# ScalarE and VectorE in the last two chunks of an expert trip: the next trip's weight units one by one

## What is computed

```python
def moe_swiglu(x, g, w_router, w_eg, w_eu, w_ed):
    h = rms_norm(x, g)
    hf = h.reshape(-1, D_MODEL)                     # (288, 1024)
    ...                                             # combine: two of eight experts per token
    for e in range(N_EXPERTS):                      # 8
        he = jax.nn.silu(hf @ w_eg[e]) * (hf @ w_eu[e])     # (., 3584)
        y = y + combine[:, e:e + 1] * (he @ w_ed[e])        # (., 1024)
    return x + y.reshape(x.shape)
```

## Time and profile before

| | |
|---|---|
| profiled execution, own time | 1645.57 us |
| its span | 1643.8 us |
| median of three runs | 1644.33 us |
| TensorE (PE) busy | 1548.1 us, 94% |
| VectorE (DVE) busy | 1243.2 us, 76% |
| ScalarE (ACT) busy | 971.6 us, 59% |
| share of PE in the chain that ended last | 85% |
| mean granted TensorE clock | 0.966 |
| expert loads (`land`, L310) | 336 of 1024 KB, median 6.0 us from issue to landing |

### The profile page before, as it was taken

The page is one execution under the profiler, slowest core; times in us unless marked ns, Lnnn a source line. Parts: engine busy times, 40 slices in busy tenths (PEclk is TensorE's granted clock), DMA queues, the critical chain, the costliest instruction groups (busy, mean ns, idle before and its releaser), DMA issues.

```text
span 1643.8 us, 22314 instructions
## 1 busy us (share of the span) xinstructions
PE 1548.1 (94%) x7942; PEld 1299.9 (79%) x7942; DVE 1243.2 (76%) x1293; ACT 971.6 (59%) x1086; POOL 87.8 (5%) x85
## 2 busy tenths in 40 slices
PE   6997999999978899989989999999998998998997
PEld 5986999999846778868868877877886887886886
DVE  6995545456774368878888878878887888887885
ACT  6554443345453446766667666667676676666674
POOL 1001110012210100000000000000000000000000
PEclk8999999999977889999999999999999999999999
DMA  8930345445340279969979969987997997997992
GB/s 330 191 96 29 128 165 180 154 167 185 114 175 1 80 274 355 360 273 377 358 276 391 356 253 393 347 340 307 339 363 291 362 363 286 370 361 262 382 357 106
DMA packets 64324, 431.40 MB, mean 262 GB/s; under 512 B 7862, under 2 KB 10166, under 8 KB 13713
## 3 DMA queue, kind: packets, MB, share of 16 engines
q1 hardware_dynamic: 57312, 412.38, 65.6%
q0 software_dynamic: 3616, 12.28, 3.2%
q10 hardware_dynamic: 3344, 6.05, 1.1%
HBM read 422.55 MB, written 9.14 MB: 263 GB/s over the span
## 4 chain that ended last, share of the span: by engine, by line
PE 85%; DVE 5%; issue 5%; ACT 3%; DMA 1%; POOL 1%; DVEq 0%; ACTq 0%; POOLq 0%
PE bank L332 25%; PE bank L334 24%; PE bank L333 24%; PE bank L370 3%; ACT w_hi L1021 2%; PE bank L722 1%; DVE w_lo L1414 1%; PE bank L354 1%; PE bank L588 1%; DVE oe_lo L1563 1%; PE bank L700 1%; PE bank L701 1%; PE bank L668 0%; PE bank L577 0%; PE bank L674 0%
## 5 line engine op out<-in xcount | busy, mean ns | idle before, releaser
L1414 DVE TENSOR_TENSOR w_lo<-land,w_hi 128x2048 fp32r<-128x2048 f32 x224 | 504.1, 2288 | 108.1 <-ACT w_hi L1021 106.5
L1021 ACT CAST w_hi<-land 128x2048 fp32r<-128x2048 f32 x224 | 417.6, 1913 | 3.5 <-issue 3.5
L332 PE MATMUL bank<-w_hi,xe_hi 128*128 128x512 f32 x896 | 370.7, 414 | 16.0 <-DVE xe_lo L1500 16.0
L333 PE MATMUL bank<-w_lo,xe_hi 128*128 128x512 f32 x896 | 358.3, 400 | 0.0
L334 PE MATMUL bank<-w_hi,xe_lo 128*128 128x512 f32 x896 | 357.8, 399 | 0.0
L1024 ACT CAST d_hi<-land 128x2048 fp32r<-128x2048 f32 x112 | 214.1, 1913 | 142.5 <-PE bank L334 142.5
L1511 DVE TENSOR_TENSOR d_lo<-land,d_hi 128x2048 fp32r<-128x2048 f32 x112 | 256.7, 2292 | 28.9 <-ACT d_hi L1024 22.3
L332 PEld LDWEIGHTS bank<-w_hi,xe_hi 128*128 128x128 f32 x896 | 170.3, 190 | 52.6 <-issue 18.5
L334 PEld LDWEIGHTS bank<-w_hi,xe_lo 128*128 128x128 f32 x896 | 170.7, 190 | 41.6
L332 PE MATMUL bank<-d_hi,heT_hi 128*128 128x512 f32 x448 | 179.9, 402 | 18.8 <-DVE heT_lo L1540 18.8
L333 PEld LDWEIGHTS bank<-w_lo,xe_hi 128*128 128x128 f32 x896 | 171.2, 191 | 32.7
(11 more groups left out here) (241 smaller groups left out, 2137.0 us busy)
## 6 DMA issues: line engine op xcount, KB each, us to landing
land<-in_w_expert SPq DMA_DIRECT2D x336, 1024.0 KB, 6.0
land<-in_w_dense SPq DMA_DIRECT2D x54, 1024.0 KB, 4.9
rel_rows<-rb POOLq DMA_DIRECT2D x1, 3072.0 KB, 35.9
bias<-rel_rows ACTq DMA_DIRECT2D x4, 512.0 KB, 4.9
X<-in_x SPq DMA_DIRECT2D x4, 288.0 KB, 5.9
out_y<-X SPq DMA_DIRECT2D x2, 576.0 KB, 4.2
Us<-in_state POOLq DMA_DIRECT2D x1, 1088.0 KB, 9.3
out_conv_s<-Us POOLq DMA_DIRECT2D x1, 1088.0 KB, 8.4
```

What stands on the lines that cost most here:

```text
L332: pe.matmul(out, w[0], x[0], start=start, stop=False)
L333: pe.matmul(out, w[0], x[1], start=False, stop=False)
L1021: act.copy(w_hi[n % RING][:], land[(DENSE + u) % LAND][:]).then_inc(hi_done, 1)
L1414: dve.tensor_tensor(w_lo[n % RING][:], land[slot][:], w_hi[n % RING][:].bitcast(F32), ALU.subtract).then_inc(split, 1)
```

## The change

In chunks 12 and 13 of a trip ScalarE and VectorE do the same operations in another order. Nothing is added or taken away.

- Unit (14,0): ScalarE makes its `hi` before `heT_hi(12)` instead of after it. On VectorE its `lo` stays behind `heT_lo(12)`.
- Unit (14,1): moved out of chunk 12 into chunk 13, behind `xe_split` and `xe_rest`.
- Unit (15,0): from behind `heT_hi(13)` and `heT_lo(13)` to ahead of them, right after (14,1).
- Unit (15,1): on ScalarE from behind `silu(14)`, the next trip's first gate, to ahead of it; on VectorE from behind `gated(14)` to ahead of it.

```diff
@@ ScalarE @@
                         with act.If(trip < n_trips - 1):
                             xe_split((trip + 1) * 2, 0)
                             xe_split((trip + 1) * 2, 1)
+                            expert_hi(trip, NCH, 1)
+                            expert_hi(trip, NCH + 1, 0)
+                    if ch + 2 == NCH:
+                        with act.If(trip < n_trips - 1):
+                            expert_hi(trip, NCH, 0)
                     act.wait_ge(heT_done, trip * NCH + ch + 1)
                     act.wait_ge(d_used, trip * NCH + ch + 2)
                     act.copy(heT_hi[:], bank[6][:, 0:CH]).then_inc(heT_hi_ready, 1)
                     if ch + 2 < NCH:
                         expert_hi(trip, ch + 2, 0)
                         expert_hi(trip, ch + 2, 1)
-                    elif ch + 2 == NCH:
+                    elif ch + 1 == NCH:
                         with act.If(trip < n_trips - 1):
-                            expert_hi(trip, ch + 2, 0)
-                            expert_hi(trip, ch + 2, 1)
-                    else:
-                        with act.If(trip < n_trips - 1):
-                            expert_hi(trip, ch + 2, 0)
+                            expert_hi(trip, NCH + 1, 1)
                             silu(trip, NCH)
-                            expert_hi(trip, ch + 2, 1)
                             expert_hi(trip, NCH, 2)
@@ VectorE @@
                             xe_rest((trip + 1) * 2, 0)
                             xe_rest((trip + 1) * 2, 1)
+                            expert_lo(trip, NCH, 1)
+                            expert_lo(trip, NCH + 1, 0)
                     dve.wait_ge(heT_hi_ready, trip * NCH + ch + 1)
                     dve.tensor_tensor(heT_lo[:], bank[6][:, 0:CH], heT_hi[:].bitcast(F32),
                                       ALU.subtract).then_inc(heT_ready, 1)
@@
                     elif ch + 2 == NCH:
                         with dve.If(trip < n_trips - 1):
-                            expert_lo(trip, ch + 2, 0)
-                            expert_lo(trip, ch + 2, 1)
+                            expert_lo(trip, NCH, 0)
                     else:
                         with dve.If(trip < n_trips - 1):
-                            expert_lo(trip, ch + 2, 0)
+                            expert_lo(trip, NCH + 1, 1)
                             gated(trip, NCH)
-                            expert_lo(trip, ch + 2, 1)
                             expert_down_lo(trip, NCH)
```

## The result

The changed kernel takes 1599.71 us as median of four runs (1598.93 to 1600.99); the kernel before, 1644.96 in runs beside it. The ratio is 0.9726, with a 95% interval of 0.9709 to 0.9743: 45 us, or 2.7%, faster.

What follows compares the result with a forecast made beforehand. TensorE's two waits per boundary, and the clock drops on them, bound the kernel. From 1645.6, seven boundaries save 31.3 us and eight drops 11.9: 1602.4, about 1601 from the median, stated as 1602; range 1597 to 1617.

Steps and rivals of the forecast that it cites:

- First wait gone: Ahead of `gate_up(14,0)`: both `xe_lo` halves ready before TensorE is free at 705.54, so its wait for the tokens disappears.
- (14,1) is late next, 0.2 us: VectorE's rest of (14,1) ends at 708.5; TensorE can go at 708.7, wants to at 708.48: 0.2 us new wait.
- (15,0) and (15,1) at no cost: Ahead of heT(13) and the gate: (15,0) costs nothing, with 0.26 us to spare before `down(13)`, the thinnest cover.
- Second wait 0.5 us: Ahead of `down(14)`: it starts at 720.69 against 720.0 without any wait; remaining waits are 0.2 and 0.5 us.
- Eight drops gone, 11.9 us: At TensorE's waits in the trips: all eight falls of the clock to 0.50 vanish, 8 x 1.49 = 11.9 us.
- Loads: Load queue: (2,2) goes out 6.1 us earlier; the queue's rest falls from 9.5 us a trip to some 2.
- that the drops stay: Rival on TensorE's clock: something besides the wait decides the drops, so they remain; 1614 us, chance 0.13.
- that the second wait stays: Rival at `down(14)`: the hand-over chain on VectorE loses 2 us, only the first wait goes; 1621 us, chance 0.08.
- that the loads bind: Rival on the load queue: a slow load comes 1.4 us late, 1612 us; at 358 GB/s 1615; chance 0.07.
- that `heT_lo(13)` comes late: Rival at `down(13)`: (15,0) not landed in time holds `heT_lo(13)`, making the kernel slower; 1649 us, chance 0.05.

## Why the prediction was right

It said 1602 us, 1597 to 1617; 1599.7 was measured. Point by point:

- *First wait gone.* So it is. The forecast had both halves of `xe_lo` 0.3 us and more ahead of TensorE; the second ends at 703.90, 0.41 ahead of the matmul at 704.31.
- *(14,1) is late next, 0.2 us.* It isn't: TensorE goes on at 707.25, right behind the turn. Its rest, of 2.29 us from 704.89, ends at 707.18, and the matmul starts 0.07 later. I had put 0.23 for this hand-over, read off a matmul that had been waiting, and so made a wait out of nothing; also the rest began 0.07 us before my time for it, shifted by the 1.23.
- *(15,0) and (15,1) at no cost.* Right, and thin as said: `heT_lo(13)` ends at 709.72 and `down(13)` starts without a wait at 710.14. The run with three units shows the price when the cover is gone.
- *Second wait 0.5 us.* 0.50. In sum 0.5 us remain a boundary instead of 0.7, a period is 4.66 us shorter than the undropped one before instead of 4.47.
- *Eight drops gone, 11.9 us.* Right, and shown to follow from the waits by filling them.
- *Loads.* The forecast gave them a rest of 2 us; it is 2.5. No wait of ScalarE for a landing shows. The rate over the periods is 351 to 358 GB/s, with 426 in the catching up. The Trainium skill (HBM Reference, Specifications (TRN2)) gives 358 GB/s for a core when both cores of a domain stream, by which I had worked out 1615. It did not bind this core, as 426 shows; no run here has both cores of a domain at work.

The sum by the trace: 7 x 4.66 = 32.6 and 11.9 for the drops, 44.5 of the 45.7 us between the two profiled executions. The other 1.2 us lie ahead of the first boundary, where `down(12)` ends 1.23 us earlier, though no instruction that TensorE waits for has moved there. They are luck and not the change. The first trip starts while the clock is still at 0.50; the windows from its first matmul to the clock's return, before and after, are:

```profile
581.09:585.99 4.90, 4.90 (x12) 3.88 (x13) 2.89 (x2) 1.35 (x2) 0.00 (x0) 0.50 0.94 366
580.67:583.75 3.08, 3.08 (x7) 2.48 (x8) 2.89 (x2) 1.36 (x2) 0.00 (x0) 0.50 0.86 330
```

The trip starts 0.42 us earlier, and the clock comes back 3.08 us into it instead of 4.90, which makes the stretch up to `down(12)`'s last matmul 123.41 us instead of 124.22. Run again, the changed kernel has 4.09 and 123.83 us. Over all twelve profiles the return lies 2.94 to 5.36 us into the trip, and this stretch grows with it from 123.33 to 124.42 us, whatever the kernel. In the first run with (15,2) moved the return came at 5.36, which makes 1.0 us more than in the changed kernel's profile and fits its gain of less than 2.5 us.

The rivals: that the drops stay, that the second wait stays, that the loads bind, and that `heT_lo(13)` comes late each had their row in the profile, and none shows it. Two of these waits were made to happen by an edit: the second one with (15,1) behind the gate, 24.6 us over the changed kernel where 1626 was expected and 1624.3 came, and a late `heT_lo(13)` with three units ahead, 15 us, near the lower end of the 1613 to 1624 expected.

## What to carry to other kernels

Where one engine waits at two places of a boundary and its helpers idle between them, look for work of the next stage that fits the idle stretch, and place it in whole pieces by the time at which each piece is first needed: two units fitted here, a third cost 15 us, and one piece on the wrong side of a wait on ScalarE undid the whole second half. Two repairs can be worth more than their sum: each alone left a wait that went on lowering TensorE's clock. A quick test of that is to fill the wait with matmuls nobody reads.

## What was not expected of the hardware

How often the clock fell behind a wait changed much with small differences of the wait. In the kernel before, waits of 2.2 and 2.5 us gave eight drops of 3.4 us in 14 waits; one wait of 2.2 us a trip gave seven in seven, one of 2.5 to 2.6 us six in seven and seven in seven; one of 1.75 us, one in seven; one of 1.5 us none in seven. The periods without a drop repeat to 0.1 us in each kernel, and those of the kernel before go by the number of drops in them: 130.41 twice with none, 131.9 and 132.0 with one, 133.3 and 133.4 with two. Its spread was the clock alone. Why two waits a trip gave fewer drops for each wait than one a trip is open.
